# Three edits in a two-block transformer kernel: the order of a weight product, the experts' down product, and the last two experts' rows

## The chip, the cores and the metric

The kernel runs on one core of a Trainium2 chip. The metric is the device time of one execution in microseconds (us); the number given for a kernel is the median of its runs.

## The reference

The input is one sequence of 512 tokens of width 1024, in float32. The first block has two layers. Each computes `x + mix(norm(x)) @ w_out`, where the mixer joins a gated recurrence (4 heads), a Fourier mixer and a dilated attention (8 heads), and then a feed-forward part `x + relu(h @ w_up)**2 @ w_down` with 4096 hidden columns. The second block has one layer: an RWKV-7 recurrence and a causal latent attention, merged by gates, and then a mixture of experts. The core of that last part is

```python
g_sel = argmax(softmax(h @ w_group + b_group))            # one group of 4
top_v, top_i = top_k(fine[g_sel], 2)                      # two of its 8 experts
gate = softmax(top_v) * gate_g
y[token] += gate * ((silu(x @ w_gate[e]) * (x @ w_up[e])) @ w_down[e])   # for both experts e
out = rmsnorm(x + y)
```

So 1024 pairs of token and expert are spread over 32 experts with 256 hidden columns each, about 32 pairs to an expert.

## The kernel before, in words

**Engines.** Each of five engines runs one program in its written order; they meet at semaphores only. A named event is counted up with `did` and waited for with `at`. PE multiplies, ACT and DVE copy, split and combine, POOL gathers, scatters and adds, and the queue SP issues most transfers.

**Split products.** A float32 weight matrix arrives in chunks of 1 MB (128 x 2048) in `raw`, a ring of two. A chunk is two units of 128 x 1024. ACT writes a unit's rounded high part to `WH` (`act_hi`, float32r), and DVE writes the rest to `WL` (`dve_lo`); `WH` and `WL` hold three units. The activations are split in the same way (`HH`, `HL`). PE then does three products in place of one: high by high, high by low and low by high. A unit's place is free when the event that `used` names has come: for most units `w_use`, for the last unit of a product, and for both units of a product of the kind "rows", `lin_mm`.

**The products of kind "rows"** (`pe_rows`, L564) give their result with tokens on the partitions. There are four in each of the two mixers: `head[4]`, and the last three of `tail`. For each of the four blocks of 128 tokens (`tk`) they go through both units of the chunk, so the second unit is wanted after 12 matrix multiplications, and neither unit is free before the end of the product.

**The mixers.** The order of PE, ACT and DVE is woven from two streams by a string of letters: `u` is one step of `win_pe`, `win_act`, `win_dve` (the products, the Fourier part, the attention) and `c` is one step of the recurrence (`rec_pe`, `rec_act`, `rec_dve`). PE uses the string `MIX_PE`, ACT, DVE and POOL use `MIX`. In the recurrence's last level, ACT's step for `hp == 0` first does two exponentials ("te") that wait for DVE and POOL, and after them copies blocks of scores. The attention (`att_pe`, `att_act`, `att_dve`) runs over 16 pairs of scores, p = 0 to 15, in a pipeline of three stages: DVE takes the row minimum of pair p, ACT its exponential, DVE normalizes pair p - 1, PE transposes pair p - 2. In `four_act` and `four_dve`, between pair 0 and pair 1, `first_units` splits the first two units of the next product's weights (`out[0]`).

**The experts.** In iteration x, PE does the up product of expert x (24 multiplications, float32r, split weights in `mo.WH`, `mo.WL`, four units each), transposes the gathered tokens of expert x + 1, does the down product of expert x - 1, and transposes the hidden rows of expert x ("ht"). The down product takes weights straight from the ring (`ring_moe`, six slots of 1 MB) and the hidden rows from `mo.hT`, both in float32: two halves (n) of 512 columns, in each two multiplications (kt). The profile shows each of those as two instructions. ACT splits the next weights (`high`), takes the sigmoid, the high part of the tokens (`turned`), half 0 of the result times the gate value (into `mo.Y`) and the copy `hT`; DVE has the low parts, the product of the gates (`hu`), and half 1 of the result. POOL gathers the tokens of expert x + 2 and scatters the rows of expert x - 1 to `ydram`, whose row 2t or 2t + 1 belongs to token t. SP refills a slot when its last reader is done; for a down chunk that is PE's down product (`sp_expert`).

**The end.** After expert 31, SP waits until the rows of experts 29, 30 and 31 have landed, each engine reads a flag (`over`, a value load) that says whether an expert had more than 128 rows, and SP reads `ydram` back in four tiles of 128 tokens (1 MB each, `mo.Y2`). DVE adds a tile's two rows for k = 0, 1 (POOL for k = 2, 3) and the residual `mo.Xr[k]`; ACT takes the square sum and its root; DVE scales, and SP writes the tile out.

## Time and profile before

| what | us |
|---|---|
| median of 3 runs (lowest, highest) | 2272.48 (2270.16, 2273.47) |
| the profiled execution's own time | 2275.16 |
| its span in the trace | 2273.4 |
| PE busy | 2159.3 |
| DVE busy | 1289.8 |
| ACT busy | 905.9 |
| POOL busy | 202.5 |

The span is what the trace covers; the own time is 1.8 us longer, for what lies around it. Busy time is the union of an engine's instructions, so matrix multiplications that overlap in the pipeline are not counted twice; the mean of one instruction is longer than the distance from one start to the next. Stretches of the span: the first block's mixers lie at 0 to 285 us and about 685 to 925 us, its feed-forward parts behind each, the second block's mixer at about 1370 to 1880 us, and the experts at 1916 to 2242 us.

### The profile page before, as it was taken

To read this page: it belongs to the slowest core of one execution; us is meant where nothing else is said; L and a number is where in the kernel's file an instruction comes from. 1 tells how busy PE (TensorE), PEld (TensorE's weight loads), DVE (VectorE), ACT (ScalarE), POOL (GpSimd) and SP (SyncE) were. 2 spreads that over 40 slices of the span, in tenths; PEclk is the share of its full clock that TensorE was granted. 3 is DMA by queue.
4 is the path that set the end of the run, shared out by engine and by line. 5 is a ranking of instruction groups with operands and counts; after the bars stand their busy time and mean duration, and the time that the engine had idled before them with its cause. 6 is when DMAs were issued, how large, how long until landed. Compare 5 with 4: busy or idle time off the path is not lost.

```text
span 2273.4 us, 32526 instructions
## 1 busy us (share of the span) xinstructions
PE 2159.3 (95%) x13880; PEld 1667.6 (73%) x13880; DVE 1289.8 (57%) x1925; ACT 905.9 (40%) x1343; POOL 202.5 (9%) x163
## 2 busy tenths in 40 slices
PE   8988999999999898999999998998999998999994
PEld 6776688888888785788888874666888467677672
DVE  8775655335447756464255454766433355777775
ACT  5444633223334337422123341344222134666662
POOL 1220000000001210100000200000000010222221
PEclk9999999999999999999999999998999998999997
DMA  4222022232222221222232222111111343899884
GB/s 182 66 79 75 20 93 93 94 106 96 93 93 75 73 73 38 75 93 93 95 109 94 93 75 90 56 56 57 60 70 46 111 188 122 312 343 357 336 339 163
DMA packets 54773, 271.53 MB, mean 119 GB/s; under 512 B 13153, under 2 KB 13409, under 8 KB 26081
## 3 DMA queue, kind: packets, MB, share of 16 engines
q1 hardware_dynamic: 44832, 260.13, 31.9%
q0 software_dynamic: 9216, 8.42, 1.1%
q8 instruction: 111, 1.82, 0.3%
q10 hardware_dynamic: 576, 0.87, 0.1%
q14 instruction: 38, 0.30, 0.0%
HBM read 264.12 MB, written 26.21 MB: 128 GB/s over the span
## 4 chain that ended last, share of the span: by engine, by line
PE 86%; DVE 8%; ACT 4%; issue 1%; DMA 1%; SPq 0%; POOLq 0%; DVEq 0%; ACTq 0%
PE psum L123 83%; PE psum L126 3%; DVE A_mix L136 2%; ACT A_mix L130 1%; DVE WL L136 1%; DVE A_second L136 1%; ACT WH L130 1%; ACT A_mix L133 1%; DVE A_second L144 1%; DVE A_moe L136 0%; DVE A_mix L156 0%; DMA A_moe<-y_rows 0%; DVE A_mix L162 0%; DVE A_moe L144 0%; DVE A_second L150 0%
## 5 line engine op out<-in xcount | busy, mean ns | idle before, releaser
L136 DVE TENSOR_TENSOR WL<-raw,WH 128x1024 fp32r<-128x1024 f32 x236 | 299.1, 1269 | 393.7 <-ACT WH L130 393.6
L130 ACT ACTIVATE WH<-raw 128x1024 fp32r<-128x1024 f32 x236 | 248.0, 1054 | 391.0 <-PE psum L123 379.1
L123 PE MATMUL psum<-HH,WH 128*128 128x512 f32 x736 | 301.3, 409 | 20.5 <-DVE HL L144 10.3
L123 PE MATMUL psum<-R_op,WH 128*128 128x512 f32 x1024 | 316.0, 390 | 0.0
L123 PE MATMUL psum<-R_ffn,WH 128*128 128x512 f32 x1024 | 315.4, 389 | 0.0
L123 PE MATMUL psum<-HH,WL 128*128 128x512 f32 x736 | 290.1, 394 | 0.0
L123 PE MATMUL psum<-HL,WH 128*128 128x512 f32 x736 | 290.0, 394 | 0.0
L123 PEld LDWEIGHTS psum<-R_op,WH 128*128 128x128 f32 x1024 | 192.2, 188 | 40.8 <-issue 1.0
L123 PEld LDWEIGHTS psum<-R_ffn,WH 128*128 128x128 f32 x1024 | 192.2, 188 | 40.1
L123 PE MATMUL psum<-R_ffn,WL 128*128 128x512 f32 x512 | 199.2, 389 | 0.0
L123 PE MATMUL psum<-R_op,WL 128*128 128x512 f32 x512 | 199.2, 389 | 0.0
L123 PEld LDWEIGHTS psum<-HH,WH 128*128 128x128 f32 x736 | 140.3, 191 | 66.9 <-DVE WL L136 13.6
L123 PE MATMUL psum<-R_moe 128*128 128x512 f32 x768 | 185.3, 397 | 2.4 <-DVE R_moe L136 1.5
L136 DVE TENSOR_TENSOR R_moe<-ring_moe,R_moe 128x1024 fp32r<-128x1024 f32 x128 | 153.5, 1220 | 58.4 <-ACT R_moe L130 55.6
L123 PE MATMUL psum<-A_second 64*64 64x64 f32 (+4 forms) x3736 | 159.0, 237 | 9.1 <-ACT A_second L132 2.7
L123 PEld LDWEIGHTS psum<-R_moe 128*128 128x128 f32 x768 | 143.0, 190 | 32.2 <-ACT R_moe L130 1.9
L123 PEld LDWEIGHTS psum<-HH,WL 128*128 128x128 f32 x736 | 139.9, 190 | 30.4
L123 PEld LDWEIGHTS psum<-HL,WH 128*128 128x128 f32 x736 | 140.2, 191 | 29.0 <-issue 1.9
L130 ACT ACTIVATE R_moe<-ring_moe 128x1024 fp32r<-128x1024 f32 x128 | 135.7, 1062 | 56.2 <-PE psum L123 55.5
L123 PEld LDWEIGHTS psum<-A_second 64*64 64x64 f32 (+3 forms) x3736 | 127.7, 139 | 39.8 <-issue 24.1
L123 PE MATMUL psum<-A_mix 128*64 128x128 f32 (+4 forms) x1408 | 128.8, 320 | 16.3 <-DVE small L162 9.5
L130 ACT ACTIVATE A_second<-psum 128x512 f32<-128x512 f32 (+3 forms) x101 | 48.0, 493 | 200.5 <-PE psum L123 186.6
(197 smaller groups left out, 2892.6 us busy)
## 6 DMA issues: line engine op xcount, KB each, us to landing
ring_moe<-in_w_gu SPq DMA_DIRECT2D x64, 1024.0 KB, 9.7
raw<-in_w_in SPq DMA_DIRECT2D x41, 1024.0 KB, 5.0
raw<-in_w_up SPq DMA_DIRECT2D x32, 1024.0 KB, 4.9
raw<-in_w_down SPq DMA_DIRECT2D x32, 1024.0 KB, 4.9
ring_moe<-in_w_dn SPq DMA_DIRECT2D x32, 1024.0 KB, 7.4
raw<-in_w_out SPq DMA_DIRECT2D x12, 1024.0 KB, 4.9
kept<-A_second SPq DMA_DIRECT2D x20, 256.0 KB, 2.2
A_mix<-A_mix SPq DMA_DIRECT2D x64, 64.0 KB, 2.0
```

Source lines behind the costliest of these rows:

```text
L123: return self.raw.matmul(o, l, r, start=start, stop=stop)
L126: return self.raw.matmul(o, i, ident, is_transpose=True, start=True, stop=True)
L130: return self.raw.activation(o, i, f, scale=scale)
L133: return self.raw.activation(o, i, f, scale=scale, bias=bias, accum_out=accum)
L136: return self.raw.tensor_tensor(o, a, b, op)
L144: return self.raw.scalar_tensor_tensor(o, a, s, b, op0, op1)
```

## The change

- `pe_rows` goes through the first unit for all four token blocks, then through the second; the first is free at `w_use`. `MIX_PE` has one more `u` ahead of the first `c` and one fewer between two later ones.
- ACT's "te" exponentials move from `hp == 0` to `hp == 1` of the recurrence's last level.
- `first_units` moves from before pair 1 of the attention to after pair 3.
- The first half of the down product's inner dimension (kt = 0) becomes three float32r products: ACT makes the high part of the weights (`mo.DH`, in the memory of X) and of the hidden rows (`mo.hTh`), DVE the low parts (`mo.DL`, `mo.hTl`). kt = 1 stays in float32. ACT now scales both halves of the result.
- Experts 30 and 31 are not scattered. Their scaled rows are split (`mo.Yh`, `mo.Yl`) and put at their tokens by a product with a one-hot matrix (`mo.at_tok`), tile by tile, for k = 2, 3 with the residual as one more product; `ydram` is zeroed ahead by 16 transfers of 256 KB from an array of zeros. SP reads the tiles back once experts 27, 28 and 29 have landed, into slots of the ring.
- PE reads the flag at expert 2, DVE before expert 0; ACT does one square root after expert 31, which loads that table.

```diff
--- before.py
+++ after.py
...
             l = lin_of_chunk[units[u][0]]
-            if l.kind == "rows" or units[u] == (l.chunks[-1], 1):
+            if units[u] == (l.chunks[-1], 1):
                 return at("lin_mm", l.n, 1)
             return at("w_use", u)
...
-            for tk in range(4):
-                if tk % 2 == 0:
-                    clear(e, l, tk // 2)
-                o = bank_of(l, tk // 2)[:, tk % 2 * 256:(tk % 2 + 1) * 256]
-                for h in range(2):
-                    e.wait_ge(*at("w_lo", u0 + h))
-                    wh, wl = unit(u0 + h)
-                    for k in range(4):
-                        xh, xl, made = operand(l, h * 4 + k)
-                        e.wait_ge(*at(*made))
-                        xh, xl = xh[:, tk * 128:(tk + 1) * 128], xl[:, tk * 128:(tk + 1) * 128]
-                        ws = slice(k * 256, (k + 1) * 256)
-                        e.mm(o, xh, wh[:, ws], h + k == 0, False)
-                        e.mm(o, xl, wh[:, ws], False, False)
-                        t = e.mm(o, xh, wl[:, ws], False, h + k == 4)
-                if tk % 2:
-                    t.then_inc(*did("lin_mm", l.n, tk // 2))
-                yield
+            for h in range(2):
+                e.wait_ge(*at("w_lo", u0 + h))
+                wh, wl = unit(u0 + h)
+                for m in range(2):
+                    if h == 0:
+                        clear(e, l, m)
+                    for tk in (2 * m, 2 * m + 1):
+                        o = bank_of(l, m)[:, tk % 2 * 256:(tk % 2 + 1) * 256]
+                        for k in range(4):
+                            xh, xl, made = operand(l, h * 4 + k)
+                            e.wait_ge(*at(*made))
+                            xh, xl = xh[:, tk * 128:(tk + 1) * 128], xl[:, tk * 128:(tk + 1) * 128]
+                            ws = slice(k * 256, (k + 1) * 256)
+                            e.mm(o, xh, wh[:, ws], h + k + tk % 2 == 0, False)
+                            e.mm(o, xl, wh[:, ws], False, False)
+                            t = e.mm(o, xh, wl[:, ws], False, h + k + tk % 2 == 5)
+                    if h:
+                        t.then_inc(*did("lin_mm", l.n, m))
+                    elif m:
+                        t.then_inc(*did("w_use", u0))
+                    yield
...
                             e.act(x.Ed[dr], x.Ed[dr], ACT.Exp).then_inc(*did("rec_act", ly, "e", l + 1, dr))
-                    elif hp == 0:
+                    elif l == 6 and hp:
                         e.wait_ge(*at("rec_dve", ly, "te"))
                         e.act(x.Ed[0], x.Ed[0], ACT.Exp).then_inc(*did("rec_act", ly, "te", 0))
...
             next(first_step)
-            first_units(e, x.out[0], act_hi)
             for d in range(2):
...
         def four_dve(e, x, first_step):
             yield
             next(first_step)
-            first_units(e, x.out[0], dve_lo)
+            next(first_step)
             yield
...
             yield from four_act(e, x, att)
-            yield from att
+            for i, _ in enumerate(att):
+                if i == 2:
+                    first_units(e, x.out[0], act_hi)
+                yield
...
             yield from four_dve(e, x, att)
-            yield from att
+            for i, _ in enumerate(att):
+                if i == 1:
+                    first_units(e, x.out[0], dve_lo)
+                yield
...
         MIX = "u" * 12 + "c" + "uu" + "cucuu" * 8 + "cuu" * 4 + "cuuuc"
-        MIX_PE = "u" * 15 + "c" + "cucuu" * 8 + "cu" + "cuu" * 3 + "cuuuc"
+        MIX_PE = "u" * 16 + "c" + "cucuu" * 8 + "cu" * 2 + "cuu" * 2 + "cuuuc"
...
-        mo.Y2 = [ar.take(2 * D) for _ in range(4)]
-        mo.O = [ar.take(D) for _ in range(4)]
-        mo.junk = ar.take(D)
+        mo.Y2 = [RX[:, k * SLOT:(k + 1) * SLOT] for k in range(4)]
+        mo.O = [RX[:, 4 * SLOT + k * D:4 * SLOT + (k + 1) * D] for k in range(4)]
+        mo.junk = A_moe[:, 2 * D:3 * D]
+        LATE = (30, 31)
+        mo.at_tok = [R_moe[:, i * S:(i + 1) * S] for i in range(2)]
+        mo.Yh, mo.Yl = mo.WH[0:2], mo.WL[0:2]
+        mo.late, mo.first_tok = mo.t2[:, 0, 0:2], [mo.t2[:, 1, 4 * i:4 * i + 4] for i in range(2)]
...
                 e.wait_ge(*at("mo_act", "ht", x))
+                e.wait_ge(*at("mo_dve", "hl", x))
+                e.wait_ge(*at("mo_dve", "dl", x))
+                hh, hl, wh, wl = (y[x % 2] for y in (mo.hTh, mo.hTl, mo.DH, mo.DL))
                 for n in range(2):
-                    b = bank()
-                    for kt in range(2):
-                        t = e.mm(b, mo.hT[x % 2][:, kt * 128:(kt + 1) * 128],
-                                 w[:, kt * 1024 + n * 512:kt * 1024 + (n + 1) * 512], kt == 0, kt == 1)
+                    b, cs = bank(), slice(n * 512, (n + 1) * 512)
+                    e.mm(b, hh, wh[:, cs], True, False)
+                    e.mm(b, hl, wh[:, cs], False, False)
+                    e.mm(b, hh, wl[:, cs], False, False)
+                    t = e.mm(b, mo.hT[x % 2][:, 128:256], w[:, 1024 + n * 512:1024 + (n + 1) * 512], False, True)
                     if n == 0:
...
                 if x:
                     down(x - 1)
+                if x == 2:
+                    many = over(e)
...
             down(31)
-            ov_pe(e)
+            ov_pe(e, many)
+            for k in range(4):
+                for n in range(2):
+                    o, cs = bank(), slice(n * S, (n + 1) * S)
+                    for i, x in enumerate(LATE):
+                        e.wait_ge(*at("mo_dve", "at_tok", i))
+                        e.wait_ge(*at("mo_dve", "yl", x, n))
+                        p = mo.at_tok[i][:, k * 128:(k + 1) * 128]
+                        e.mm(o, p, mo.Yh[i][:, cs], i == 0, False)
+                        t = e.mm(o, p, mo.Yl[i][:, cs], False, i == 1)
+                        if i == 0 and k >= 2:
+                            e.wait_ge(*at("mo_act", "xr", k, n))
+                            e.mm(o, ident, mo.Xr[k][:, cs], False, False)
+                    t.then_inc(*did("mo_pe", "late", k, n))
...
+            def late(x):
+                for n in range(2):
+                    _, b = turn.next()
+                    e.wait_ge(*at("mo_pe", "dn" if n else "y0", x))
+                    e.act(mo.Yh[x - LATE[0]][:, n * S:(n + 1) * S], b, ACT.Copy, mo.gsl[:, x:x + 1]).then_inc(
+                        *did("mo_act", "yh", x, n))
...
             def down(x):
-                n, b = turn.next()
...
-                e.act(mo.Y[x % NB][:, 0:S], b, ACT.Copy, mo.gsl[:, x:x + 1]).then_inc(*read("mo_act", turn, n))
+                if x in LATE:
+                    return late(x)
+                for i in range(2):
+                    n, b = turn.next()
+                    e.wait_ge(*at("mo_pe", "dn" if i else "y0", x))
...
+                    e.act(mo.Y[x % NB][:, i * S:(i + 1) * S], b, ACT.Copy, mo.gsl[:, x:x + 1]).then_inc(*read("mo_act", turn, n))
                 mark("mo_act", "y", x)
...
+            def down_high(x):
+                w, loaded = xslot("dn", x, 0)
+                e.wait_ge(*loaded)
+                e.wait_ge(*(at("mo_pe", "dn", x - 2) if x >= 2 else at("mo_pe", "xr", 3, 1)))
+                e.act(mo.DH[x % 2], w[:, 0:UNIT], ACT.Copy).then_inc(*did("mo_act", "dh", x))
...
+                if x:
+                    down_high(x - 1)
...
+                if x == 31:
+                    down_high(31)
...
+                e.act(mo.hTh[x % 2], b[:, 0:128], ACT.Copy)
+                e.act(mo.hT[x % 2][:, 128:256], b[:, 128:256], ACT.Copy).then_inc(*did("mo_act", "ht", x))
             down(31)
+            e.act(mo.rr[:, 0:1], eps, ACT.Sqrt)
             ov_act(e)
             for k in range(4):
...
+                    e.wait_ge(*at("mo_act", "yh", x, n))
+                    e.stt(mo.Yl[i][:, cs], b, mo.gsl[:, x:x + 1], mo.Yh[i][:, cs].bitcast(F32), MUL, SUB).then_inc(
+                        *read("mo_dve", turn, k))
...
+            def places():
+                for i in range(2):
+                    r = mo.first_tok[i]
+                    step(e.ts(r, c("tok"), c("tok")[:, 0:1], mo.late[:, i:i + 1], SUB, SUB), "ft", i, 0)
+                    step(e.ts(r, r, -1.0, None, MUL), "ft", i, 1)
+                e.wait_ge(*at("mo_pe", "up", LATE[0]))
+                for i in range(2):
+                    e.tt(t3(mo.at_tok[i], 4), bcast(c("io128"), 1, 4), bcast(mo.first_tok[i], 2, 128), ALU.is_equal).then_inc(
+                        *did("mo_dve", "at_tok", i))
+
+            def tile_sum(k):
+                y = mo.Y2[k][:, 0:D]
+                e.wait_ge(*at(f"Y{k}"))
+                e.tt(y, y, mo.Y2[k][:, D:2 * D], ADD).then_inc(*did("mo_dve", "ys", k))
+                if k < 2:
+                    e.wait_ge(*last("mo_dve"))
+                    e.wait_ge(*at("mo_act", "xr", k, 1))
+                    e.tt(y, y, mo.Xr[k], ADD).then_inc(*did("mo_dve", "yx", k))
...
                 turn.next()
-                n, b = turn.next()
-                e.wait_ge(*at("mo_pe", "dn", x))
...
-                e.ts(mo.Y[x % NB][:, S:2 * S], b, mo.gsl[:, x:x + 1], None, MUL).then_inc(*read("mo_dve", turn, n))
-                mark("mo_dve", "y", x)
+                turn.next()
...
+            def turned_low(x, n, b):
+                if x >= 2:
+                    e.wait_ge(*at("mo_pe", "dn", x - 2))
+                e.wait_ge(*at("mo_act", "ht", x))
+                e.tt(mo.hTl[x % 2], b[:, 0:128], mo.hTh[x % 2].bitcast(F32), SUB).then_inc(*read("mo_dve", turn, n))
+                mark("mo_dve", "hl", x)
+
+            def down_low(x):
+                w, _ = xslot("dn", x, 0)
+                e.wait_ge(*at("mo_act", "dh", x))
+                e.tt(mo.DL[x % 2], w[:, 0:UNIT], mo.DH[x % 2].bitcast(F32), SUB).then_inc(*did("mo_dve", "dl", x))
...
+                if x:
+                    turned_low(x - 1, *hidden)
+                    down_low(x - 1)
...
+                else:
+                    down_low(31)
+                if x == 31:
+                    places()
...
                 if x:
                     down(x - 1)
-                turn.next()
+                hidden = turn.next()
+            turned_low(31, *hidden)
+            tile_sum(0)
             down(31)
-            ov_dve(e)
+            for k in range(1, 4):
+                tile_sum(k)
+            ov_dve(e, many)
...
                 if k < 4:
-                    y = mo.Y2[k][:, 0:D]
-                    if k < 2:
-                        e.wait_ge(*at(f"Y{k}"))
-                        step(e.tt(y, y, mo.Y2[k][:, D:2 * D], ADD), "y", "sum", k)
-                    else:
-                        e.wait_ge(*at("mo_pool", "ys", k))
-                    e.wait_ge(*at("mo_act", "xr", k, 1))
-                    e.tt(y, y, mo.Xr[k], ADD).then_inc(*did("mo_dve", "y2", k))
+                    e.wait_ge(*last("mo_dve"))
+                    for n in range(2):
+                        _, b = turn.next()
+                        y = mo.Y2[k][:, n * S:(n + 1) * S]
+                        e.wait_ge(*at("mo_pe", "late", k, n))
+                        t = e.tt(y, y, b, ADD)
+                    t.then_inc(*did("mo_dve", "y2", k))
                 if k:
...
                 sp_chunk(e, n)
+                z = n - mixes[0].ffn.half[0][0][0].chunks[0]
+                if 0 <= z < 16:
+                    e.dma(ydram[z * 64:(z + 1) * 64, :], I["zero"]).then_inc(*sent("zero", z))
...
-            for x in (31, 30, 29):
+            for x in (27, 28, 29):
                 e.wait_ge(*at(f"y{x % NB}", x))
+            for k, free in enumerate((("mo_dve", "w", 123), ("mo_pe", "dn", 29), ("mo_dve", "w", 125), ("mo_dve", "w", 127))):
+                e.wait_ge(*at(*free))
+                e.dma(mo.Y2[k], y_tile(k)).then_inc(*sent(f"Y{k}"))
             ov_sp(e)
-            for k in range(4):
-                e.dma(mo.Y2[k], ydram[k * 256:(k + 1) * 256, :].rearrange("(p r) n -> p (r n)", r=2)).then_inc(*sent(f"Y{k}"))
             for k in range(4):
                 e.wait_ge(*at("mo_dve", "out", k))
                 e.dma(out[k * 128:(k + 1) * 128, :], mo.O[k]).then_inc(*sent("out", k))
...
```

## Rows read from the trace of the kernel before

**Rows 1.** The page: span, busy time, chain by engine.

```profile
span 2273.4 us, 32526 instructions
PE 2159.3 (95%) x13880; PEld 1667.6 (73%) x13880; DVE 1289.8 (57%) x1925; ACT 905.9 (40%) x1343; POOL 202.5 (9%) x163
PE 86%; DVE 8%; ACT 4%; issue 1%; DMA 1%; SPq 0%; POOLq 0%; DVEq 0%; ACTq 0%
```

**Rows 2.** Waits of PE over the whole span (engine, line, what it waited for: us, times, longest).

```profile
PE psum L123 <- DVE WL L136: 15.0, 5, 4.7
```

**Rows 3.** Timeline, PE in the mixers (start, duration, engine, line, operation, output, inputs).

```profile
67.83 0.39 PE L123 MATMUL psum<-WH,HH 128*128 128x256 f32 x1 [2.09 <-DVE WL L136]
...
132.08 1.16 PE L123 MATMUL psum<-A_mix 64*128 64x128 f32 x16 [1.20 <-DVE A_mix L156]
...
145.83 0.58 PE L123 MATMUL psum<-WH,HH 128*128 128x256 f32 x1 [4.21 <-DVE WL L136]
...
148.68 2.08 PE L123 MATMUL psum<-A_mix 64*128 64x128 f32 x16
...
795.46 0.58 PE L123 MATMUL psum<-WH,HH 128*128 128x256 f32 x1 [4.72 <-DVE WL L136]
```

**Rows 4.** Windows (stretch; busy PE, PEld, DVE, ACT, POOL; clock; DMA share; GB/s), first mixer.

```profile
130.00:165.00 35.00, 29.27 (x211) 26.40 (x211) 21.25 (x26) 18.75 (x32) 7.62 (x6) 0.90 0.31 91
```

**Rows 5.** Timeline at the start of the second layer's attention.

```profile
857.49 1.99 ACT L130 ACTIVATE WH<-raw 128x1024 fp32r<-128x1024 f32 x2
...
858.56 2.36 DVE L136 TENSOR_TENSOR WL<-raw,WH 128x1024 fp32r<-128x1024 f32 x2 [3.78 <-ACT WH L130]
...
860.84 1.28 DVE L136 TENSOR_TENSOR HL<-psum,HH 128x512 fp32r<-128x512 f32 x2
...
863.39 2.08 PE L123 MATMUL psum<-A_mix 64*128 64x512 f32 x4 [4.76 <-DVE small L162]
...
865.40 1.97 PE L126 MATMUL psum<-C,A_mix 128*128 128x128 f32 x8
```

**Rows 6.** Timeline, PE and ACT over one expert.

```profile
2214.74 3.60 PE L123 MATMUL psum<-ring_moe,A_moe 128*128 128x512 f32 x8
...
2218.31 5.75 PE L123 MATMUL psum<-R_moe 128*128 128x512 f32 x24
...
2220.05 1.06 ACT L130 ACTIVATE R_moe<-ring_moe 128x1024 fp32r<-128x1024 f32 x1 [1.07 <-PE psum L123]
...
2223.90 1.04 PE L126 MATMUL psum<-C,A_moe 128*128 128x128 f32 x8
...
2224.77 3.60 PE L123 MATMUL psum<-ring_moe,A_moe 128*128 128x512 f32 x8
```

**Rows 7.** Windows, experts 3 to 29.

```profile
1938.00:2210.00 272.00, 272.00 (x1141) 190.90 (x1140) 201.27 (x245) 180.48 (x244) 70.20 (x54) 1.00 0.89 340
```

**Rows 8.** Waits of the queue SP in 1938 to 2230 us.

```profile
SPq L168 <- PE psum L126: 254.7, 29, 9.0
```

**Rows 9.** DMA issues in 1938 to 2210 us (size each, median us to landing).

```profile
ring_moe<-in_w_gu SPq DMA_DIRECT2D x56, 1024.0 KB, 9.7
```

**Rows 10.** Timeline, the end of the kernel.

```profile
2233.91 3.59 PE L123 MATMUL psum<-ring_moe,A_moe 128*128 128x512 f32 x8
...
2240.28 0.69 ACT L130 ACTIVATE A_moe<-psum,A_moe 128x512 f32<-128x512 f32 x1 [2.14 <-PE psum L123]
...
2243.58 0.98 POOL L175 DMA_INDIRECT y_rows<-A_moe  x1 [3.48 <-DVE A_moe L140]
...
2247.41 2.06 SPq L168 DMA_DIRECT2D A_moe<-y_rows  x4
...
2252.26 2.48 DVE L136 TENSOR_TENSOR A_moe<-A_moe 128x1024 f32<-128x1024 f32 x2 [9.51 <-DMA A_moe<-y_rows]
...
2258.02 5.62 POOL L136 TENSOR_TENSOR A_moe<-A_moe 128x1024 f32<-128x1024 f32 x2 [13.46 <-DMA A_moe<-y_rows]
...
2268.99 1.29 DVE L144 SCALAR_TENSOR_TENSOR A_moe<-A_moe,raw 128x1024 f32<-128x1024 f32 x1
```

65 lines of the change are left out of this document (39 added, 26 removed).

## The prediction

> **What bounds the kernel now.** I read the page first: PE is busy for 95% of the span and 86% of the chain that ended last is PE's [rows 1]. So what counts is PE's own work, PE's pauses, and the end, where PE has nothing left to do. Then PE's waits: the largest is for low parts of weights, 15.0 us in 5 waits [rows 2]. The timeline places them [rows 3]: 2.09 us at 67.83 and 4.72 us at 795.46, with partners of 2.09 us at 716.95 and 4.21 us at 145.83. These four (13.1 us) stand before multiplications of 256 columns, products of the kind "rows". The long ones have a second cost: 16 transposed score products take 1.16 us at 132.08, but 2.08 us at 148.68, after the pause [rows 3], and the windows give a mean granted clock of 0.90 over 35 us [rows 4]. With the two levels 1.2 and 2.4 GHz that is 7.0 us at the lower one. The attention's start has a wait of 4.76 us, in both layers alike [rows 5]. Among the experts PE never pauses (272.00 of 272.00 us busy, clock 1.00), while DVE is busy for 201.27 us and ACT for 180.48 us [rows 7]. The end, from the last down product on, is transfers and a chain over DVE, ACT and POOL [rows 10].
>
> **1. Order of the "rows" products.** The second unit is wanted after 48 multiplications instead of 12. At some 0.12 us each at the full clock that is 4.3 us more cover against waits of 2.1 to 4.7 us; ACT's earlier splitting (it no longer stands behind the "te" exponentials) covers the rest. All four waits go: -13.1. The two long ones take the lower clock with them: 7.0 us at half rate is at most 3.5 us lost, of which some is pause counted already; I take 2.8 each, -5.6. Bounds: 0 and -7.
>
> **2. MIX_PE and "te".** PE comes to each step of the recurrence one product step (24 multiplications, some 3 us) later. The wait of 1.20 us at 132.08 [rows 3], its twin in layer 2 (1.19) and two at the first mixer's head (1.00, 0.29) are on DVE and have this cover: 3.7 us at most, I take -1.8. The later "te" makes DVE's products of the last level later; they feed PE two steps on. What is late next is ACT and DVE as a whole, since PE arrives sooner everywhere; no row prices that. Bounds 0 and 13 (all the waits come back), I take +3, nearer 0 because DVE idles for over a third of those stretches [rows 4].
>
> **3. Units of `out` later.** Before, ACT (1.99 us) and DVE (2.36 us) split them ahead of pair 1, and DVE's row minimum of pair 1 waits until 862.04, behind HL at 860.84; PE's next scores start at 863.39, at the lower clock (2.08 and 1.97 us for steps that take half of it later) [rows 5]. With pair 1 first, those minima run at 858.8 and PE goes on at 860.1; the transposes start near 862.5 instead of 865.40: 2.9 us, and 1 to 2.8 us of clock. But the same 2.0 us of ACT then lie in the running pipeline, where a pair takes 3.1 us and ACT is busy 2.9 of it: 1.5 to 2.5 us come back. Net -2.5 a layer, -5.0. Bounds 0 and -9.
>
> **4. The down product.** Its eight float32 passes go from 2214.74 to the next work at 2218.18: 0.43 us each, 0.86 a multiplication. The 24 float32r ones go from 2218.31 to 2223.90: 0.233 each [rows 6]. A half was 2 x 0.86 = 1.72 and becomes 3 x 0.233 + 0.86 = 1.56 us. Two halves save 0.32 us, 32 experts 10.2 us; the iteration falls from 10.03 (2214.74 to 2224.77) to 9.71 us. The Trainium skill's page FP8 and Floating Point Precision (TensorE Precision Notes) says that true FP32 takes four passes through the array. The row agrees (0.43 for two). By that count alone, a half would lose one pass of 0.215 us, which makes 13.8 us in all; the sum keeps the rows' 10.2, since float32r runs at 0.233 here.
>
> Cover for the new side work: ACT gains a split (1.0), the second half of the result (0.69, as at 2240.28 [rows 10]) and about 0.2 for the copy in two parts, so 1.9 on 180.48 / 27.1 = 6.7 us: 8.6 of 9.7. DVE gains a split (1.2) and a difference of 128 columns (0.3), loses 0.75: 7.4 + 0.8 = 8.2 of 9.7. Both fit. In order: ACT's weight split stands in the gap of about 1.1 us before `high` at 2220.05 [rows 6]; behind it wait three `high` and DVE's lows. Counted from the end of the up product, ACT's chain (result, hidden rows, split, three highs) ends at about 9.75, and the next sigmoid can start at 9.9. DVE has the low part ready at 7.9, PE wants it at 10.6. If this cover were gone, each us would cost 31. Transfers: the queue SP waits 254.7 us for PE's down products [rows 8], so slots, not bandwidth, time the loads; they land 9.7 us after issue [rows 9], and the split needs its chunk some 5 us sooner than PE did, with 3.7 us left. 340 GB/s at a share of 0.89 [rows 7] becomes 351 at 0.92.
>
> **5. Flag, zeros, table.** PE's value load in expert 2 is uncovered. No row shows one; at the end, landing of the last scatter and SP's value load together take 2.85 us (POOL done at 2244.56, SP at 2247.41) [rows 10]. Bounds 0 and 2.9, I take +1, as most of that is the landing. DVE's lies in its wait for the first gather. The 16 transfers of zeros are issued in a stretch where the queues run at a quarter of their time: 0 (if that cover is gone, one late chunk, about 1 us). POOL waits for them in expert 1, a millisecond later. The table load (1.28 us) goes under a wait.
>
> **6. The end.** From the last up product's end, 2233.68, to the span's end are 39.7 us. New, counted from there: DVE does `hu` (to 1.7), the low part of the down weights (3.2), places (four small steps, two of 0.65: 5.3), the split of expert 30's rows (6.7) and the low hidden part (7.0). The last down product starts at 7.1 instead of 4.6, and ends at 10.2. Tile reads are issued at about 0.5 (scatter of expert 29 plus 2.85), and land from 5.4 on at the old spacing of about 3 us (2247.41 to 2252.26 for the first, POOL's at 2258.02 the third [rows 10]), so by 14. DVE then: tile 0 to 9.6, expert 31's rows to 11.9, tiles 1 to 3 to 16.8, two additions of 0.7 per tile and the scaling of 1.3, up to 29.0; behind the last scaling come 3.1 us as before (2270.3 to 2273.4). End 32. PE's one-hot products (4 x 0.233 a half, with 0.86 more for k = 2, 3: 11.2 us) are done by 22, when DVE wants the last at 25. The pause of 3.3 us before the last down product may bring the lower clock: 2.7 more. I take 33: -6.7. Bounds -11 and -2.
>
> **The sum.** -13.1 - 5.6 - 1.8 + 3 - 5.0 - 10.2 + 1 - 6.7 = -38.4. The profiled execution took 2275.2 us, so 2236.8; the median shown is 2.7 lower, which gives 2234.1.
>
> **Rivals.**
> - *The waits move on.* The mixers' waits are DVE's and ACT's lateness, not the order of units, and return at the next product. For it: DVE carries rotation, recurrence and lows in the same stretch. Against it: after each wait the trace shows no other for 10 us or more. Half of parts 1 to 3 is lost: 2234 + 12 = 2246. Chance 0.15.
> - *The experts stay at 10.03 us.* ACT has about 0.1 us left in its order and DVE follows it; or transfers fill the period. Then part 4 gives nothing: 2244. Against it: every one of PE's demands has some 2.5 us behind ACT. The skill's DMA: Bandwidth & Descriptors (Specifications) gives about 358 GB/s per core; by that the period could fall to 340 x 10.03 / 358 = 9.5 us, so it does not bind; the wanted 351 is near it. Chance 0.10.
> - *More comes.* Attention and end give their upper bounds: 2222. Chance 0.08.
> - *Slower.* The weight split in front of three highs waits for its chunk's landing in each iteration, and with it the whole of ACT, DVE and PE. It decides from a landing that is 3.7 us later than now; to undo the other 28 us and more, the period must pass 10.03 + 28 / 31 = 10.9 us, a landing 4.9 us later. At 5.4 us later the period is 11.4, +43 against -28: 2289. Against it: SP's long waits [rows 8]. Chance 0.03.
> - *The change does not do what it says.* The flag path is taken, or the tiles are read after the last product: then part 6 gives 0: 2241, inside the forecast's range. Chance 0.04.
>
> **How the numbers follow.** The forecast has 0.60. Its own range is 2226 to 2243, from the bounds of parts 3, 5 and 6. To leave out no more than 2 in 10 the range must take in both 2244 and 2246 with their spread: 2221 to 2253. About 0.2% (4.5 us) can be told from no change. Slower has the 0.03 of its rival; for a sum near zero nearly all parts would have to fail: 0.02. Faster 0.95.
>
> **What would show it.** Right: no wait of PE for WL before products of 256 columns, and a clock near 1.00 in 130 to 165; no wait of 4.8 us at the attention's start, a smaller one after pair 3; starts of consecutive experts' down products 9.7 us apart, with no pause; a pause of about 3 us before the last down product; tile reads issued before that product; some 33 us from the last up product to the end. Wrong: PE waits for `down_split` or the weights' high parts in each expert, PE at the lower clock over the one-hot products so that DVE waits for them, or new waits of PE in the mixers that add up to over 5 us.

## The result, and the profile after

The changed kernel takes 2258.82 us (median of 5 runs, 2255.05 to 2262.47), the kernel before in the same comparison 2273.47 us (2270.16 to 2278.86): ratio 0.9930, 95% interval 0.9915 to 0.9944. It is faster by 15 us. The forecast was 38 us faster (2234, range 2221 to 2253), so the sign is right and the time lies above the range.

The page of the changed kernel (span; busy time by engine; chain by engine), against [rows 1]:

```profile
span 2256.8 us, 32933 instructions
PE 2161.2 (96%) x13984; PEld 1685.7 (75%) x13984; DVE 1321.1 (59%) x1976; ACT 955.7 (42%) x1442; POOL 189.6 (8%) x159
PE 85%; DVE 8%; ACT 4%; DMA 1%; issue 1%; SPq 0%; POOL 0%; DVEq 0%; POOLq 0%; ACTq 0%
```

PE's busy time is nearly what it was (2159.3), and still the span is 16.6 us shorter. Two things hide in that sum: PE has less work among the experts, and the one-hot products fill idle time at the end (from the last up product's end on PE is busy for 19.2 us, before for 7.3). To see where the time fell, I cut the spans of the two profiled executions at landmarks of PE's timeline: the attention's first products, the wait of 1.55 us near its end, and the end of the last up product.

| stretch, us | before | after | forecast for it |
|---|---|---|---|
| start to attention 1, and between the attentions | 196.3 + 581.8 | 195.6 + 584.0 | -17.5 (parts 1, 2) |
| the two attentions | 67.4 + 67.1 | 67.2 + 67.0 | -5.0 (part 3) |
| attention 2 to the last up product's end | 1321.5 | 1309.9 | -9.2 (parts 4, 5) |
| from there to the end | 39.3 | 33.2 | -6.7 (part 6) |

The last two lines came nearly as forecast, and 2.2 us of the third line's 11.6 lie ahead of the first expert's up product (1916.48 before, 1915.37 after), where the change alters none of PE's work: from there to the last up product's end it is 9.3 us. The first two lines, 22.5 us of the forecast, came to +1.2. The timeline of PE in the experts of the changed kernel, against [rows 6]:

```profile
2204.92 0.94 PE L123 MATMUL psum<-down_split,R_moe 128*128 128x512 f32 x3
...
2214.60 0.94 PE L123 MATMUL psum<-down_split,R_moe 128*128 128x512 f32 x3
```

These two start 9.68 us apart. Over the 29 steps from the down product of expert 0 to that of expert 29 the mean is 9.71 us (1932.88 to 2214.60), which is the forecast; before it was 10.02 (1934.11 to 2224.77). The windows of the mixer and of the experts (stretch; busy PE, PEld, DVE, ACT, POOL; clock; DMA share; GB/s), against [rows 4, 7], and the landing of the up weights, against [rows 9]:

```profile
130.00:165.00 35.00, 33.44 (x311) 30.68 (x312) 26.55 (x31) 19.86 (x33) 8.63 (x6) 1.00 0.33 95
1938.00:2200.00 262.00, 261.50 (x1188) 199.25 (x1187) 218.75 (x270) 217.85 (x325) 62.68 (x54) 1.00 0.92 353
```

```profile
ring_moe<-in_w_gu SPq DMA_DIRECT2D x54, 1024.0 KB, 10.8
```

In 130 to 165 us the clock is at 1.00 (0.90 before) and PE works 4.2 us more. But in 165 to 182 us, behind a new pause, it is at 0.80, where it was at 1.00 before. Among the experts PE is idle for 0.5 us in 262, and the transfers bring 353 GB/s (forecast 351). But PE's waits over the whole span, against [rows 2], say that the mixers did not become smooth:

```profile
PE psum L123 <- DVE WL L136: 12.7, 14, 1.9
...
PE psum L123 <- DVE small L162: 9.2, 6, 2.7
...
PE psum L123 <- DVE A_mix L144: 6.3, 2, 3.2
PE psum L126 <- ACT A_mix L130: 4.9, 8, 1.5
PE psum L123 <- DVE R_moe L136: 4.7, 2, 3.2
```

Five waits for WL of 15.0 us became 14 short ones of 12.7 us (one of 1.9 us, in the second block, is the same in both), and there are two new ones for A_mix, line 144 (DVE's state products). The timeline of PE in the first mixer shows them, against [rows 3]:

```profile
78.33 0.50 PE L123 MATMUL psum<-HH,WH 128*128 128x512 f32 x1 [1.34 <-DVE WL L136]
...
115.63 0.50 PE L123 MATMUL psum<-HH,WH 128*128 128x512 f32 x1 [0.80 <-DVE WL L136]
...
139.22 0.39 PE L123 MATMUL psum<-WH,HH 128*128 128x256 f32 x1 [1.17 <-DVE WL L136]
...
172.37 7.86 PE L123 MATMUL psum<-A_mix 128*64 128x128 f32 x62 [3.23 <-DVE A_mix L144]
...
210.10 1.13 PE L123 MATMUL psum<-A_mix 64*128 64x512 f32 x4 [1.40 <-DVE small L162]
212.29 1.97 PE L126 MATMUL psum<-C,A_mix 128*128 128x128 f32 x8 [1.06 <-DVE HL L136]
...
223.93 1.13 PE L123 MATMUL psum<-A_mix 64*128 64x512 f32 x4 [2.72 <-DVE small L162]
```

Most of the new waits stand before products of 512 columns, where there was none. At the attention's start the wait of 4.76 us [rows 5] is now 1.40 + 1.06, but 2.72 us come three pairs later.

### The profile page after: what moved, and what is told of

Read it like the earlier page. It is cut to its first block, busy times and chain, and to the rows that moved or that the text cites. A ratio compares the mean times of both kernels' runs of the same rounds, so it can differ in the third digit from the quotient of the medians.

```text
span 2256.8 us, 32933 instructions
## 1 busy us (share of the span) xinstructions
PE 2161.2 (96%) x13984; PEld 1685.7 (75%) x13984; DVE 1321.1 (59%) x1976; ACT 955.7 (42%) x1442; POOL 189.6 (8%) x159
## 4 chain that ended last, share of the span: by engine, by line
PE 85%; DVE 8%; ACT 4%; DMA 1%; issue 1%; SPq 0%; POOL 0%; DVEq 0%; POOLq 0%; ACTq 0%
PE psum L123 82%; PE psum L126 3%; DVE A_mix L136 2%; DVE WL L136 1%; ACT A_mix L130 1%; ACT A_mix L133 1%; DVE A_second L136 1%; DMA A_moe<-h_rows,A_moe 1%; DVE A_second L144 1%; ACT WH L130 1%; DVE A_mix L162 0%; DVE A_mix L156 0%; DMA A_mix<-A_mix 0%; DVE ring_moe L136 0%; SPq L168 0%
## 5 line engine op out<-in xcount | busy, mean ns | idle before, releaser
L123 PE MATMUL psum<-R_moe 128*128 128x512 f32 x800 | 195.0, 399 | 3.8 <-DVE R_moe L136 1.5
L123 PEld LDWEIGHTS psum<-R_moe 128*128 128x128 f32 x800 | 149.0, 190 | 37.0 <-issue 4.4
```

Of the source, the lines that this page charges most:

```text
L123: return self.raw.matmul(o, l, r, start=start, stop=stop)
```

## The experiments

Below, "first/second" are the stretches up to the first attention and between the two. The kernel before ran beside each group: 2274.1, 2272.5, 2273.7, 2274.0 and 2273.9 us. Where no range is given (m_rows, m_rows_mixpe, m_te, n_rows_te, m_units, n_oldmix_noswap) there is one execution only, and the executions of one kernel lie 4 to 14 us apart; there the waits in the trace carry the reading, more than the time. Stretches and waits are always those of one profiled execution.

**Which half of the change pays?** The changed kernel with all edits of the mixers undone (m_experts).

> The changed kernel with all its edits to the mixers undone (order of the rows products, MIX_PE, te, first_units); experts and end as changed. Both theories take the two traces' ends at their word: from the first expert's up product to the end the changed kernel is 15.5 us shorter (1916.5 to 2273.4 against 1915.4 to 2256.8), and the mixers gave 1.1. So some 2259.5 us against 2273 for the kernel before, ratio 0.993 to 0.994. If the mixers' edits were worth the 23 us forecast for them, this kernel would be slower than the changed one by far more than 1 us, at 2265 or more.

Measured: 2258.06 us (2256.57 to 2263.5), ratio 0.9938 (0.9921 to 0.9955). The experts and the end alone give the whole gain. The mixers' edits are worth nothing together: each helps nothing, or one undoes the others.

**The mixers' edits, one by one, on the kernel before.** The order of units in products of kind "rows" alone (m_rows: the new `pe_rows`, and its release of the units), and with the new MIX_PE (m_rows_mixpe):

```
-        MIX_PE = "u" * 15 + "c" + "cucuu" * 8 + "cu" + "cuu" * 3 + "cuuuc"
+        MIX_PE = "u" * 16 + "c" + "cucuu" * 8 + "cu" * 2 + "cuu" * 2 + "cuuuc"
```

> The kernel before with the rows products' new order alone (pe_rows and used). Theory A: behind about 125 us of the first mixer, DVE's order is paced by the rotation of queries and keys (swap transfers, POOL, DVE), and DVE's products that PE needs for the recurrence stand behind it; what PE saves in the rows products it waits for later. Then the span is 2271 to 2274, the waits of 4.2 and 4.7 us for WL are gone, and PE has new waits for DVE of about that size before the first mixer's attention starts (204.7 us before). Rival B: the shorter spacing in MIX_PE and the later te eat a real gain; then without them this kernel is 8 to 13 us faster than before (span 2260 to 2265).

> The kernel before with the rows products' new order and the new MIX_PE, without the later te. Theory A: as m_rows within 2 us, with a pause before the recurrence's output product of 3 us or more, since PE comes there one product step earlier. Rival B with MIX_PE as the cause: slower than m_rows by 6 us or more over both layers (3.2 and 3.1 us of pause and the lower clock each time). Rival B with te as the cause: the pause before the output product is absent here and the gain is 8 us or more.

Measured: 2264.63 us for the first (first/second 189.5/577.3 against 196.3/581.8), 2277.41 us for the second (196.3/584.1). The order of units gives 10.6 us of span, with no wait for WL left in the first block's mixers (theory A, that nothing would be gained, was wrong). MIX_PE on top takes back 12.7, as the rival that names it has it. So the edits are not idle: one takes what the other gives. The waits of DVE between 60 and 168 us, of m_rows and then of m_rows_mixpe:

```profile
DVE A_mix L156 <- PE psum L123: 9.2, 7, 2.7
```

```profile
DVE A_mix L156 <- PE psum L123: 13.6, 9, 2.7
```

DVE stands 4.4 us longer in front of PE's recurrence products. The timeline of DVE in the changed kernel shows what stands behind:

```profile
111.92 1.35 DVE L156 COPY_PREDICATED A_mix<-M,psum 128x512 f32<-128x512 uint8 x2 [2.66 <-PE psum L123]
113.17 1.27 DVE L136 TENSOR_TENSOR A_mix<-A_mix 128x512 f32<-128x512 f32 x2
114.36 1.22 DVE L136 TENSOR_TENSOR WL<-raw,WH 128x1024 fp32r<-128x1024 f32 x1
```

DVE's masked copy waits for PE until 111.92; the split of WL behind it ends at 115.58, and PE, which needs it, has waited until 115.63 (the row above). PE waits for its own lateness, by way of DVE.

**Later "te"** alone (m_te), and with the order of units (n_rows_te).

```
-                    elif hp == 0:
+                    elif l == 6 and hp:
                         e.wait_ge(*at("rec_dve", ly, "te"))
```

> The kernel before with the later te alone. Theory A: ACT splits the second unit earlier, so the waits of 4.21 and 4.72 us for WL fall to under 1 us here too, without the new order; and the span changes by less than 3 us, since the rotation sets what follows. Rival B (te is what costs): the span rises by 3 us or more.

> The kernel before with the rows products' new order and the later te, MIX_PE as before. The order alone gave a span of 2262.8, te alone 2265.1, against 2273.4. If both remove the same waits for WL (theory: one cause, two cures), the span is 2260 to 2264, little better than either. If they add, it is 2254 to 2256. The pause of 3.15 us before the recurrence's output product in the first mixer (168.75 in m_rows) is DVE's: with te later it stays at 2.5 us or more.

Measured: 2266.85 us alone (span -8.3; the waits of 4.21 and 4.72 us are 2.38 and 3.50), where the theory had waits under 1 us and a span within 3 us, and 2265.09 us with the order of units, against 2264.63 for that alone. Both treat the same waits, and their gains don't add, as the theory of the second had it.

**The changed kernel with the old MIX_PE** (n_oldmix; once more as yardstick of a later group, n_oldmix_again).

> The changed kernel with MIX_PE of the kernel before, all else as changed. Theory: MIX_PE alone takes back the mixers' gain, since PE, one product step further ahead of ACT and DVE, meets each product before its low part is made. Its cost on top of the new order was 12.7 us of span (2262.8 to 2275.5). So the span is 2242 to 2247 here, against 2256.8 for the changed kernel, ratio to before 0.986 to 0.989, and the waits of 0.5 to 1.4 us for WL in the first mixer's 78 to 139 us are gone. Rival: with te moved as well, MIX_PE costs nothing of its own; then the span stays within 3 us of 2256.8.

> The changed kernel with the kernel before's MIX_PE once more, as the yardstick for the next two in the same comparison. Theory: 2244 to 2251, with another amount of TensorE's lower clock in the mixers from run to run. Rival, that the first result was luck: nearer the changed kernel's 2259.

Measured: 2248.96 us (2246.25 to 2250.11), ratio 0.9893 (0.9876 to 0.9909), and 2248.37 us (2245.82 to 2251.5), ratio 0.9892 (0.9875 to 0.9909). Undoing one line gains 10 us, clear of both kernels' scatter, and no wait for WL is left in the first block's mixers. MIX_PE is the largest step that failed.

**By which mechanism: the orders of ACT and DVE shifted too** (p_both), PE one more step later (p_17), PE one step earlier than before (p_late14, on n_oldmix_late below).

```
+        MIX_DVE = "u" * 13 + "c" + "uu" + "cucuu" * 8 + "cuu" * 3 + "cu" + "cuuuc"
...
-                weave(MIX, u=win_act(e, x), c=rec_act(e, x))
+                weave(MIX_DVE, u=win_act(e, x), c=rec_act(e, x))
...
-                weave(MIX, u=win_dve(e, x), c=rec_dve(e, x))
+                weave(MIX_DVE, u=win_dve(e, x), c=rec_dve(e, x))
```

```
-        MIX_PE = "u" * 16 + "c" + "cucuu" * 8 + "cu" * 2 + "cuu" * 2 + "cuuuc"
+        MIX_PE = "u" * 17 + "c" + "cucuu" * 8 + "cu" * 3 + "cuu" + "cuuuc"
```

```
-        MIX_PE = "u" * 15 + "c" + "cucuu" * 8 + "cu" + "cuu" * 3 + "cuuuc"
+        MIX_PE = "u" * 14 + "c" + "cucuu" * 8 + "cuu" * 4 + "cuuuc"
```

> The changed kernel, with the order in which ACT and DVE alternate between product steps (u) and recurrence steps (c) shifted by one u as well, as MIX_PE is. Theory: MIX_PE's new order costs time because DVE, which still goes to each recurrence step after the old number of product steps, stands waiting for PE's product there (13.5 us in 9 waits between 60 and 168 us against 9.2 in 7 with the old order) with a split of low parts (WL) queued behind it. With DVE's order shifted too, DVE splits first: its waits for PE fall back to 9 us, PE's 14 waits for WL go, and the time is that of the old order, 2246 to 2252. Rival: PE has no cover for the recurrence in any order that comes later (ACT and DVE as a whole are late): 2256 to 2262 or more, with waits of PE for the recurrence's operands instead.

> The changed kernel with PE one product step later still at each recurrence step (17 u before the first c instead of 16). Theory: a dose: the step from 15 to 16 cost 12.7 us with rows alone and 10 us in the changed kernel, and this one costs as much again, 2266 to 2272, with PE's waits for WL some twice as long. Rival: the cost comes from a coincidence at 16 or is limited by something else: 2255 to 2262.

> The version with the late units of out (n_oldmix_late, 2236.2 us), with PE one product step earlier at each recurrence step (14 u before the first c instead of 15). Theory: DVE waits less for PE's recurrence products, and works off its queue earlier, but PE has to wait for DVE's operands of the recurrence in its turn, 1 to 3 us at some of 20 steps: 2236 to 2250, so 15 is near the best. Rival: the gain of the step from 16 to 15 goes on: 2226 to 2232, with less than 1 us more of PE's waits for A_mix.

Measured: p_both 2239.85 us (2234.67 to 2248.34), ratio 0.9861 (0.9833 to 0.9889); p_17 2335.9 us (2335.07 to 2340.86), ratio 1.0281 (1.0264 to 1.0298); p_late14 2241.49 us (2237.94 to 2242.73). Waits of DVE between 60 and 168 us in p_both, and of DVE in the same stretch and PE in the span of p_17:

```profile
DVE A_mix L156 <- PE psum L123: 8.0, 6, 2.7
```

```profile
DVE A_mix L156 <- PE psum L123: 43.6, 12, 7.0
```

```profile
PE psum L123 <- DVE WL L136: 69.1, 25, 5.4
```

With ACT and DVE shifted too (POOL keeps its order), the new MIX_PE costs nothing: PE is busy for 79.91 of the 80 us from 50 to 130 (75.96 in the changed kernel), and its waits for WL fall from 12.7 to 2.5 us. The time is 9 us under that of the old order, below the theory's 2246 to 2252; its own executions lie 14 us apart, and q_both_late below repeats no such gain, so I don't count it. The two edits move ACT and DVE together: that it is DVE's place in the order and not ACT's is read from the timeline above, not tested alone. With PE alone one step further off, the loop between the two queues closes at many more steps: 25 waits of 69.1 us, where the changed kernel has 14. The theory's mechanism holds; its dose (10 us more) was far too small; that the first step had used up what cover there was is my reading of it. The step to the other side makes PE wait 4.29 us at the first recurrence step (58.25, for A_mix), where its base waits 2.04, and takes away the base's wait of 2.4 us for A_mix of line 144. The time, 5 us above that of the base, can't be told from it: the two ranges overlap.

**Is it the distance, or the recurrence's own lateness?** All three orders one more step later (q_both2_late), beside all three once (q_both_late, the best guess at a full version), both with the units of `out` late. In q_both2_late MIX_PE is that of p_17, and ACT, DVE and POOL have:

```
-        MIX = "u" * 12 + "c" + "uu" + "cucuu" * 8 + "cuu" * 4 + "cuuuc"
+        MIX = "u" * 14 + "c" + "uu" + "cucuu" * 8 + "cuu" * 2 + "cu" * 2 + "cuuuc"
```

> The changed kernel with the orders of ACT and DVE shifted by one u as well (p_both, 2239.9 us) and with the first units of out split near the attention's end (which gave 12 us beside the old MIX_PE). Theory: the two gains lie in other stretches, so the waits add up: 4 to 5 us a layer at the attention on top, 2227 to 2233. Rival: part of the 12 us was another draw of TensorE's lower clock, or the late split's ACT work collides with the product after the attention: 2234 to 2242.

> As q_both_late, but with all three engines (PE, ACT, DVE) one more product step later at each recurrence step: 17 u for PE, 14 for ACT and DVE before the first c. Theory: p_17 was slow (2335.9) because only PE was shifted; with the others shifted as well the distance between them is that of the kernel before, so its 77 us go, and the time is within 10 us of q_both_late. Rival: a recurrence that comes 2 u later is itself too late for the end of the product (the rotations and states behind it): over 2250.

Measured: 2236.74 us (2234.33 to 2240.8), ratio 0.9839 (0.9824 to 0.9854), and 2253.63 us (2250.2 to 2258.71), ratio 0.9912 (0.9897 to 0.9926). The first is what its rival had (2234 to 2242): the gains of p_both and of the late units don't add, and the time is that of the late units beside the old MIX_PE (2236.2, below). In the second the 77 us of p_17 are gone, so the distance between the queues is what it paid for; but the recurrence's lateness has a price of its own, 17 us, which I had put at under 10. PE's timeline in q_both2_late has it before the output products:

```profile
172.52 7.78 PE L123 MATMUL psum<-A_mix 128*64 128x128 f32 x52 [6.48 <-DVE A_mix L144]
```

In q_both_late that wait is 3.03 us.

**The units of `out`.** Part 3 alone on the kernel before (m_units), part 3 undone beside the old MIX_PE (n_oldmix_units), and the split moved to the attention's end (n_oldmix_late):

```
-                if i == 2:
+                if i == 15:
                     first_units(e, x.out[0], act_hi)
...
-                if i == 1:
+                if i == 14:
                     first_units(e, x.out[0], dve_lo)
```

> The kernel before, with part 3 alone: the first units of out split at pairs 1 and 2 of the attention instead of ahead of pair 1. The prediction gave it -5.0 us (2.5 a layer). Theory now, from the timelines (the start's wait of 4.76 us falls to 1.40 + 1.06, but a wait of 2.3 to 2.7 for small comes after the split): it is a shift of one wait, worth 0 to -2 us in both layers together, so 2270 to 2275. Rival (the prediction): 2267 to 2269.

> The changed kernel with the kernel before's MIX_PE and with the first units of out split ahead of pair 1 again (part 3 undone). Theory: part 3 only shifts the wait, so 0 to +2 us against the kernel with the old MIX_PE alone, and a wait of 4.8 us at the attention's start with none of 2.3 after pair 3. Rival (the prediction's -2.5 a layer): +5.

> The changed kernel with the kernel before's MIX_PE, and the first units of out split near the attention's end (at its pairs 14 and 15), where the running pipeline has to find 2 us of ACT once. Theory: the same 2 us of ACT come back there as one wait of about 2.3 us instead of the one after pair 3, so 0 +- 1.5 us. Rival: near the end the split is hidden, no wait takes its place, and both layers give 2 to 3 us each, so -4 to -6.

Measured: 2274.65 us (attentions 67.4 and 65.7, before 67.4 and 67.1); 2248.63 us (2244.49 to 2249.21) against the yardstick's 2248.37; and 2236.2 us (2232.18 to 2241.75), ratio 0.9832 (0.9813 to 0.9851). Part 3 as made is worth nothing that can be told; at the end of the attention the medians differ by 12 us, and there my theory was wrong. Both attentions take 62.9 us instead of 67.0 and 67.1. PE's timeline at the attention's start of n_oldmix_late (no wait of 2.3 to 2.7 us is left), and ACT's at its end:

```profile
208.01 1.14 PE L126 MATMUL psum<-C,A_mix 128*128 128x128 f32 x8 [0.29 <-ACT A_mix L130]
209.09 2.15 PE L123 MATMUL psum<-A_mix 128*64 128x128 f32 x20
211.17 1.09 PE L126 MATMUL psum<-C,branch_gates 128*128 128x128 f32 x8
212.19 2.15 PE L123 MATMUL psum<-A_mix 128*64 128x128 f32 x20
```

```profile
253.22 0.60 ACT L130 ACTIVATE A_mix<-psum 128x512 f32<-128x512 f32 x1 [0.33 <-PE psum L126]
253.71 1.99 ACT L130 ACTIVATE WH<-raw 128x1024 fp32r<-128x1024 f32 x2
255.93 0.60 ACT L130 ACTIVATE A_mix<-psum 128x512 f32<-128x512 f32 x1 [0.23 <-PE psum L126]
```

The 1.99 us of splits lie behind the last exponentials, where ACT waits for PE anyway. They lie behind the attention's landmark too, and something comes back there: in layer 2 a new wait of 0.57 us for A_mix, in layer 1 the lower clock (16 products in 1.98 us at 253.11, 1.09 before). From the landmark to the next product's start are 6.60 and 5.81 us, against 5.04 and 5.05 in n_oldmix_again, so 5.9 of the attentions' 8.2 us remain. The two profiled executions differ by 7.1 us in all, not by the medians' 12: there are 5.7 us less in the first stretch (188.7 against 194.3), where the edit changes nothing, and 4.7 and 2.0 us more in the two stretches behind the attentions, what comes back among them. The split's own share is thus about 6 us; the rest of the 12 isn't explained by it, and the last section has a likely reason.

**The pause before the output product** (n_oldmix_noswap). This kernel leaves out the swap of halves in the rotation, 64 transfers, so queries and keys are not rotated; the routing, and with it the experts' work, is another, and only the mixers can be read.

```
-                for q in range(4):
-                    to, of = 32 * q, 32 * (q ^ 1)
-                    e.dma(x.sw[i % 2][to:to + 32, :], src[of:of + 32, :]).then_inc(*sent(f"sw{i % 2}", l.ly, i, q))
...
-            e.wait_ge(*at(f"sw{i % 2}", x.ly, i, 3))
...
-                e.wait_ge(*at(f"sw{i % 2}", x.ly, i, 3))
...
-                e.tt(x.sw[i % 2], x.sw[i % 2], x.turn[1], MUL).then_inc(*did("rot_dve", x.ly, "s", i))
+                if i >= 2:
+                    e.wait_ge(*at("rot_dve", x.ly, "a", i - 2))
+                e.tt(x.sw[i % 2], x.turn[0], x.turn[1], MUL).then_inc(*did("rot_dve", x.ly, "s", i))
```

> n_oldmix without the 64 transfers that swap halves of queries and keys for the rotation (DVE multiplies two tables in their place, so the queries and keys are other numbers; the work of DVE and POOL is the same). Theory: the pause of about 3 us before the recurrence's output product comes from DVE's in-order wait for those transfers: it is gone or under 1 us, and the span falls by 3 us or more, up to 8 with the clock. Rival: DVE's amount of work there or te sets it: the pause stays over 2 us and the span within 2 us of n_oldmix.

Measured: 2240.22 us; first/second 186.1/571.8 against 190.4/578.5 of n_oldmix. The waits of 2.75 and 2.27 us for line 144 are gone. So that pause hangs on the swap's transfers: DVE's state products are queued behind rotation steps that wait for them. POOL's wait for the same transfers goes with the edit, so the two are not told apart.

**The end** (n_oldmix_tail): DVE works off the hidden rows of expert 31 before it makes places and splits expert 30's rows.

```
-                if x == 31:
-                    places()
...
             turned_low(31, *hidden)
+            places()
+            late(30, held)
```

> n_oldmix, and at expert 31 DVE makes the low part of the hidden rows ahead of the one-hot matrices and of the split of expert 30's rows. In the changed kernel PE paused 3.23 us before the last down product for it, and ran at the lower clock for some 3 us after. If that pause is on the path to the end: 1.5 to 4 us less than n_oldmix. If DVE's own queue (tile sums, additions, scaling) sets the end, since the same work only changes its order: within 1 us of it.

Measured: 2245.22 us (2238.4 to 2250.37), ratio 0.9882 (0.9864 to 0.9900), not told apart from n_oldmix. The pause before the last down product fell from 3.23 to 1.38 us, but PE still paused 2.96 us before the one-hot products (2.79 and 3.40 us in n_oldmix's two profiles), and the end took 32.3 us (31.9 and 33.7 in n_oldmix's two profiles). The pause was not on the path to the end; DVE's own chain was, as the second theory had it.

## Why the prediction was wrong

By the runs, about 11 of the 22 us that are missing from the span are MIX_PE's, 8 are part 1's and 5 part 3's; against these stand the 2 us of the stretch that the change leaves alone.

**Part 2, MIX_PE: the largest step that failed.** The prediction took +3 between bounds of 0 and 13, "nearer 0 because DVE idles for over a third of those stretches", against -1.8 of cover. Measured on top of the other order: +12.7 (10 in the changed kernel), its upper bound. DVE's idle time was no slack: DVE was idle at the head of its queue, waiting for the very products that MIX_PE made later, with the splits behind. The prediction asked what PE would find ready, not which queue waits for PE. The condition named under "Wrong", new waits in the mixers of over 5 us, is what came; the rival "the waits move on" (2246, 0.15) is nearest in kind, but took half the gain where all of it went.

**Part 1, the order of "rows" products**: in m_rows the four waits and the low clock in 130 to 165 went as forecast (in the changed kernel five short waits of 4.0 us stand before such products, with the new MIX_PE), but -18.7 measured -10.6 alone, and -10.2 with the later "te". The step that fell short is "all four waits go" as a gain: PE comes earlier and then waits 3.15 and 2.44 us for A_mix of line 144, which hang on the swap's transfers (n_oldmix_noswap); in layer 2 the lower clock comes behind (the 80 output products take 8.30 us there, 6.82 in layer 1). This was in no term of the sum, though "what is late next" had been asked.

**Part 3**: -5.0 measured -0.6 alone and 0 beside the others. The mechanism was right (start earlier, 2 us of ACT come back in the running pipeline), the size of what comes back was not. In the changed kernel PE reaches the split 3.4 and 4.2 us earlier, counted from the scores ahead of the old wait of 4.76 us, near the 3.9 to 5.7 forecast; but 3.1 and 4.0 us came back where 1.5 to 2.5 were allowed: waits of 2.72 and 2.30 us, and in layer 2 products at the lower clock behind the wait.

**Part 4**: right, 9.71 us forecast and measured; ACT and DVE had room (each busy for 8.1 of a period's 9.7 us), PE paused once for 0.5 us, and the weights landed in 10.8 us. The mean period fell by 0.31 us, 9.9 us for 32 experts, where the rows' durations gave 10.2. The Trainium skill, FP8 and Floating Point Precision (TensorE Precision Notes), has four passes for true FP32; by passes alone that would have made 13.8 us, an estimate that the runs don't bear out.

**Part 5**: no cost of the flag or the zeros could be read; **part 6**: right, 33.5 us against 33 forecast and 39.7 before by the prediction's count (from the start of the last up multiplication; 33.2 and 39.3 in the table above), with the pause of 3.23 us and the lower clock behind it. Its one-hot products add up to 10.9 us, not the 11.2 written, and nothing hung on it. Part 5's "the table load goes under a wait" failed. ACT's timeline in the changed kernel:

```profile
2235.63 1.28 ACT L130 ACT_TABLE_LOAD   x1
...
2237.13 1.28 ACT L133 ACT_TABLE_LOAD   x1
...
2243.64 1.28 ACT L132 ACT_TABLE_LOAD   x1
```

The load and one root ahead (2235.63) don't last: the square sums (line 133) have a load of their own at 2237.13, the root has another at 2243.64, and DVE's reciprocal waits 1.51 us for it. Behind that third load, squares and roots of the other tiles alternate with no further load (2245.32 to 2252.30); why the second load stands there isn't shown. The Trainium skill, ScalarE: Activation LUTs (What ACT_TABLE_LOAD costs), gives about 1283 ns for a load; the trace agrees with 1.28 us.

**The sum.** The forecast of parts 4 to 6, -15.9, came as -15.5 from the first expert's up product on (-9.3 and -6.2). Parts 1 to 3, -22.5, came as +1.2, and 2.2 us fell between attention 2 and the experts, for no reason that the change gives. With MIX_PE undone the change gives 25 us, with the split at the attention's end too 37 us, which is the forecast's size, but by another way than its own, and partly by luck (n_oldmix_late, above).

## What to carry to other kernels

An in-order engine that idles at a wait has no slack for the work queued behind that wait: before one engine's order is moved, look at who waits for what it moves, and what stands behind it there. Orders written by hand for several engines are moved together or not at all; here one step of PE's alone cost 10 to 13 us, a second one 77 more, and one step of PE's, ACT's and DVE's together cost nothing. Side work in a pipeline that is full goes to where the pipeline drains, not a few steps further on. Removed waits are worth what is left after the next one.

## What the runs showed of the hardware

The same pause doesn't always bring the lower clock. These are windows of 165 to 182 us of m_rows, then of n_oldmix_again, each followed by the row of the recurrence's output products; both have a pause of about 3 us before these products:

```profile
165.00:182.00 17.00, 13.86 (x138) 10.39 (x136) 9.53 (x19) 4.91 (x9) 2.33 (x2) 1.00 0.35 124
```

```profile
168.75 6.82 PE L123 MATMUL psum<-A_mix 128*64 128x128 f32 x80 [3.15 <-DVE A_mix L144]
```

```profile
165.00:182.00 17.00, 14.35 (x97) 8.89 (x96) 8.85 (x19) 3.21 (x8) 1.70 (x1) 0.60 0.35 124
```

```profile
168.08 11.75 PE L123 MATMUL psum<-A_mix 128*64 128x128 f32 x80 [2.65 <-DVE A_mix L144]
```

The mean clock is 1.00 in one and 0.60 in the other, and the 80 products behind the pause take 6.82 and 11.75 us, though the longer pause is the first one's. In n_oldmix, the same kernel as n_oldmix_again, they take 8.28 us after 2.75 us of pause, and the first attention starts at 190.4 instead of 194.3 us. This is likely what spreads the times of one kernel over 4 to 14 us, as much as many of the edits tried here are worth: the four executions of p_both took 2234.67, 2236.32, 2243.38 and 2248.34 us at mean granted clocks of 0.988, 0.987, 0.984 and 0.981. I had reckoned each pause's clock as a fixed term. The Trainium skill's page TensorE: Matmul & The Clock Gate (What's actually happening) says that the chip's look at PE's activity runs freely and does not start with the kernel; that would let one pause end either way, and the runs agree, but none isolates it.
